# A decaying head's sum of squares by two products of rounded operands instead of one in fp32, one slot later

## The reference

```python
def _hgrn2(q_raw, f_raw, i, lb, o_g):
    q = jax.nn.silu(q_raw)
    logf = jnp.log(lb + (1.0 - lb) * jax.nn.sigmoid(f_raw))
    k = (1.0 - lb) * jax.nn.sigmoid(-f_raw)
    ...                                   # scan over chunks: o = inter + intra
    o = _rms(o, o_g)                      # o * rsqrt(mean(o * o over the head's 128) + 1e-6) * o_g
    return o
...
hg = _hgrn2(g_q, g_f, g_i, lbs[l], hg_norm_g[l]) * jax.nn.silu(g_z)
```

## Time and profile before

| | |
|---|---|
| median of three runs | 2654.63 us |
| profiled execution, its own time | 2656.35 us |
| its span, first to last instruction | 2655.04 us |
| mean granted TensorE clock, share of full | 0.997 |
| busy share: TensorE products | 99% |
| busy share: TensorE weight loads | 79% |
| busy share: VectorE | 37% |
| busy share: ScalarE | 41% |
| busy share: GpSimd | 44% |

### The profile page before, as it was taken

The page is one execution under the profiler, slowest core; times in us unless marked ns, Lnnn a source line. Parts: engine busy times, 40 slices in busy tenths (PEclk is TensorE's granted clock), DMA queues, the critical chain, the costliest instruction groups (busy, mean ns, idle before and its releaser), DMA issues.

```text
span 2655.0 us, 34587 instructions
## 1 busy us (share of the span) xinstructions
PE 2621.5 (99%) x14142; PEld 2101.7 (79%) x14142; DVE 970.0 (37%) x1584; ACT 1094.4 (41%) x1781; POOL 1162.1 (44%) x590
## 2 busy tenths in 40 slices
PE   7999999999999999999999999999999999999999
PEld 4577778778888888878887777777888888888887
DVE  3535544333334231244676333334332233321300
ACT  5335344434444442244444444445444444433311
POOL 0024344344444454453344444445555556554543
PEclk9999999999999999999999999999999999999999
DMA  9942333233333224422222323332333333333443
GB/s 386 351 156 96 103 103 106 85 122 107 115 115 106 89 99 156 146 91 80 88 80 80 104 93 103 99 107 92 105 114 115 113 108 117 115 117 110 139 146 107
DMA packets 102253, 322.92 MB, mean 122 GB/s; under 512 B 11472, under 2 KB 13264, under 8 KB 101584
## 3 DMA queue, kind: packets, MB, share of 16 engines
q1 hardware_dynamic: 98208, 307.06, 35.0%
q10 hardware_dynamic: 3888, 13.66, 1.3%
HBM read 303.90 MB, written 16.78 MB: 121 GB/s over the span
## 4 chain that ended last, share of the span: by engine, by line
PE 96%; DMA 2%; ACT 0%; DVE 0%; SPq 0%; issue 0%; POOL 0%; DVEq 0%; ACTq 0%
PE bank L813 29%; PE bank L815 28%; PE bank L814 28%; DMA TA<-in_w_ada 2%; PE bank L1020 1%; PE bank L1009 1%; PE bank L713 1%; PE bank L940 1%; PE bank L1003 1%; PE bank L974 1%; PE bank L1055 1%; PE bank L1069 0%; PE bank L880 0%; PE bank L866 0%; PE bank L1047 0%; PE bank L867 0%
## 5 line engine op out<-in xcount | busy, mean ns | idle before, releaser
L2131 POOL TENSOR_TENSOR wlo<-wraw,whi 128x1024 fp32r<-128x1024 f32 (+3 forms) x430 | 992.0, 2308 | 1358.3 <-ACT whi L1124 1357.8
L813 PE MATMUL bank<-Hhi,whi 128*128 128x512 f32 x2848 | 1147.9, 403 | 3.1 <-DVE Y L1686 1.5
L814 PE MATMUL bank<-Hlo,whi 128*128 128x512 f32 x2848 | 1111.6, 390 | 0.0
L815 PE MATMUL bank<-Hhi,wlo 128*128 128x512 f32 x2848 | 1111.5, 390 | 0.0
L1124 ACT ACTIVATE whi<-wraw 128x1024 fp32r<-128x1024 f32 (+3 forms) x454 | 457.3, 1008 | 661.0 <-PE bank L815 635.7
L813 PEld LDWEIGHTS bank<-Hhi,whi 128*128 128x128 f32 x2848 | 535.0, 188 | 132.8 <-issue 22.3
L815 PEld LDWEIGHTS bank<-Hhi,wlo 128*128 128x128 f32 x2848 | 534.7, 188 | 114.8
L814 PEld LDWEIGHTS bank<-Hlo,whi 128*128 128x128 f32 x2848 | 535.5, 188 | 107.5 <-issue 2.4
L813 PE MATMUL bank<-Ohi,whi 128*128 128x512 f32 x320 | 128.0, 400 | 0.0
L815 PE MATMUL bank<-Ohi,wlo 128*128 128x512 f32 x320 | 124.8, 390 | 0.0
L814 PE MATMUL bank<-Olo,whi 128*128 128x512 f32 x320 | 124.7, 390 | 0.0
(11 more groups left out here) (270 smaller groups left out, 2549.7 us busy)
## 6 DMA issues: line engine op xcount, KB each, us to landing
wraw<-in_w_in SPq DMA_DIRECT2D x304, 512.0 KB, 3.5
TA<-in_w_ada SPq DMA_DIRECT2D x64, 512.0 KB, 7.4
wraw<-in_w_out SPq DMA_DIRECT2D x32, 512.0 KB, 3.5
wraw<-in_w_o SPq DMA_DIRECT2D x32, 512.0 KB, 3.5
wraw<-in_w_mem ACTq DMA_DIRECT2D x16, 512.0 KB, 7.0
Y<-in_w_ada SPq DMA_DIRECT2D x16, 512.0 KB, 4.4
first<-in_w_ada SPq DMA_DIRECT2D x16, 512.0 KB, 4.6
tmp_mgs<-TA SPq DMA_DIRECT2D x32, 256.0 KB, 2.2
```

Of the source, the lines that this page charges most:

```text
L813: e.matmul(out, hi[:, c], xhi[k], start=first and j == 0, stop=False)
L814: e.matmul(out, hi[:, c], xlo[k], start=False, stop=False)
L815: m = e.matmul(out, lo[:, c], xhi[k], start=False, stop=last and end)
L2131: e.tensor_tensor(M.wlo[b][:, 0:w], M.wraw[b][:, 0:w], M.whi[b][:, 0:w].bitcast(F32), ALU.subtract).then_inc(S.lo)
```

## The change

The squares in `hg_sq` are copied by ScalarE into a rounded high part, `hg_hi`, in slot 10; VectorE subtracts it from them in slot 11, in place, to make `hg_lo`; and TensorE sums both parts with the rounded ones into the same bank in slot 12. Ln, Exp and VectorE's two products move to slot 12 too, and `hg` has 12 rests on the other engines. The high part lies in the `ST` buffer of the head's half, so the next writers of that buffer get waits: `decay` of head h waits for the sum of head h - 2, and SyncE's strips 0 and 1 wait for the sums of heads 6 and 7, where they waited for the last multiplications of heads 6 and 7.

```diff
+        self.hg_hi, self.hg_lo = pieces(TR, 6144, 2), TR[:, 4864:5376]
...
# tensor_program, hg
             yield
-            pe.wait_ge(S.hgq, h + 1)
+            yield
+            pe.wait_ge(S.hgd, h + 1)
             pe.wait_ge(*free[BS0])
-            e.matmul(M.bS0, ones, M.hg_sq, start=True, stop=True).then_inc(S.hgs)
+            e.matmul(M.bS0, one, M.hg_hi[b], start=True, stop=False)
+            e.matmul(M.bS0, one, M.hg_lo, start=False, stop=True).then_inc(S.hgs)
...
# scalar_program, hg
         e.activation(M.hg_sq, M.bO, ACT.Square).then_inc(S.hgq)
+        act.wait_ge(S.hgq, h + 1)
+        e.activation(M.hg_hi[h % 2], M.hg_sq, ACT.Copy).then_inc(S.hgh)
+        yield
         yield
         act.wait_ge(S.hgs, h + 1)
...
# vector_program, decay
             dve.wait_ge(S.t2e, t2 - 1)
+            if h > 1:
+                dve.wait_ge(S.hgs, h - 1)
             e.tensor_scalar(F, M.t2, a, M.par[:, 56 + h:57 + h], ALU.mult, ALU.add).then_inc(S.dec)
...
# vector_program, hg
         yield
+        dve.wait_ge(S.hgh, h + 1)
+        e.tensor_tensor(M.hg_lo, M.hg_sq, M.hg_hi[b].bitcast(F32), ALU.subtract).then_inc(S.hgd)
+        yield
         y = M.y[8 + h]
...
# gpsimd_program
-        gates=gates, hg=idle(11), ...
+        gates=gates, hg=idle(12), ...
...
# sync_program
     def hg(h):
         if h == 7:
-            sp.wait_ge(S.hgu, 9 * 7)
+            sp.wait_ge(S.hgs, 7)
             strip(1, 0)
-        return rest(11)
+        return rest(12)
...
             if which == 1 and h < 7:
-                sp.wait_ge(*((S.s1, 4 * h) if h else (S.hgu, 9 * 8)))
+                sp.wait_ge(*((S.s1, 4 * h) if h else (S.hgs, 8)))
                 strip(1, h + 1)
```

More of the change, by code:

```diff
@@ L433, in __init__ @@
         self.hgo, self.hgq, self.hgs, self.hgl, self.hgr = sem("hgo"), sem("hgq"), sem("hgs"), sem("hgl"), sem("hgr")
+        self.hgh, self.hgd = sem("hgh"), sem("hgd")
         self.y = sem("y")
@@ L2250, in gpsimd_program @@
         setup=setup, mem=mem, mem_kv=idle(3), mem_turn=idle(2), ada=nothing, sums=nothing, gain=nothing, h_put=h_put,
-        gates=gates, hg=idle(11), attend=attend, window=window, put=put, x_load=nothing, h2=h2, index=idle(3), topk=idle(48), mix_load=nothing, out_load=nothing, end=nothing,
+        gates=gates, hg=idle(12), attend=attend, window=window, put=put, x_load=nothing, h2=h2, index=idle(3), topk=idle(48), mix_load=nothing, out_load=nothing, end=nothing,
         part=part, out=out, posts=dict(
```

## The result

The changed kernel takes 2659.41 us (median of 20 runs, 2656.12 to 2663.13); the kernel before, run beside it, 2656.30 us (20 runs, 2654.04 to 2658.95). The ratio is 1.0013, with a 95% interval of 1.0007 to 1.0019. I had forecast 2651.7 us, 0.11% less than the 2654.63 us of three earlier runs of the kernel before; what its 20 runs show is 1.7 us above these three, so the forecast is compared by the difference: 2.9 us less forecast, 3.1 us more measured. The changed kernel's profiled execution has a span of 2659.1 us, 4.1 us more than that of before.

What follows compares the result with a forecast made beforehand. TensorE, busy 99% of the span, was taken as the bound. Seven heads saving 0.42 us each, head 7's saving lost, gave 2.9 us off 2654.63: 2651.7 us, 0.11% less; range 2650.5 to 2655.8.

Steps and rivals of the forecast that it cites:

- The step moved by one slot: `hg`, 12 rests for 11: heads 0 to 3 start 0 to 3 slots later, from head 4 only the last step shifts; cost zero.
- The saving of the products: TensorE, eight heads: fp32 sum costs 0.87 us, the rounded pair 0.45; 0.42 us saved each, 3.4 us in all.
- The chain of the remainder: Heads 4 to 6: remainder follows Square, Copy and decay tail; head 4's done at 416.2, TensorE at 416.50, no wait.
- what I said of the cover: Square, Copy and remainder have two slots (5.2 us) of cover; with one (2.73 us) every head would wait.
- Head 7: Later Ln delays the remainder of ak's norm (L1798); TensorE waits at L866, so head 7's 0.42 us saving is gone.
- The waits of decay and of SyncE: New waits of VectorE's L1784 and SyncE's strips for earlier heads' sums: zero cost.
- The rival with GpSimd: Heads 4 to 6: remainder falls behind GpSimd's subtraction, TensorE waits 3.1 us each; 2660.9 us. Chance 0.05, half collision 0.08.
- the lost saving: Rival: the pair costs what the fp32 sum did, through changing forms; 2654 to 2655 us. Chance 0.06.

Runs made afterwards that it cites:

- the experiment: The whole change without its extra slot (remainder in slot 10, pair in slot 11, 11 rests), against the kernel before: 2652.39 us, ratio 0.9984.

## Why the prediction was wrong

**The step that failed** is "The step moved by one slot", with its end "Nothing to pay". It had the new starts of heads 0 to 3 right (0, 1, 2 and 3 slots later), and then looked only at the bank that the next head needs. For the moved last step I asked what it would now stand behind on each engine's queue. For the steps in slots 0 to 10 of heads 1 to 3, which move too, I did not ask it. Those steps are links of a chain between TensorE and VectorE: each of VectorE's multiplications has to be done before TensorE comes to the next slot. The shift put them behind other work of VectorE and under GpSimd's subtraction. "From head 4 on nothing shifts but the last step" was right by the count of slots, and yet head 4 has a wait of 1.0 us, since head 3 now ends right ahead of it. What the step put at nothing cost 5.7 us of waits and 1.6 us of half clock in the profile, and 7.5 us of stage when the empty slot was tried alone.

**The saving of the products** was right: 0.42 us each forecast, 0.45 measured, 3.6 us in all eight where I had 3.4. The 131 ns of the Trainium skill ("TensorE: Matmul & The Clock Gate", "Back-to-back issue gap") are again not what the trace shows (0.23 us, 235.10 to 235.33).

**The chain of the remainder** in heads 4 to 6 was right: for head 4 I had its start 4.3 us after the Square and found 4.20 (416.82 to 421.02), and TensorE did not wait. GpSimd's subtraction began 1.07 us behind it (422.09), where I had said 1.0 us of room. All eight remainders took 0.69 us; none fell under GpSimd:

```profile
L1950 DVE TENSOR_TENSOR TR<-TA,TR x8: 684/688/693, 231.8 to 579.2; 128x512 fp32r<-128x512 f32 x8
```

**But what I said of the cover was wrong**: "if it were one (2.73 us) every head would wait". With one slot no head waits. The rows give it: Square, Copy and remainder took 1.98 us from the first start to the last end in the experiment (408.30 to 410.28), and the slot comes 2.53 us after the Square's start. I had counted the three operations and not set their sum against one slot.

**Head 7** came as worked out. Its pair is at 583.20; L1955 follows at 2.04 us (2.06 forecast), L1808 at 3.44 (3.5), L869 at 4.18 (4.2), a wait of about 1.0 us for TensorE where it had been 0.6:

```profile
583.20 0.39 PE L985 MATMUL bank<-TR,one 128*128 128x512 f32 x1
585.24 0.75 DVE L1955 SCALAR_TENSOR_TENSOR Y<-bank,cst,TA 128x512 f32<-128x512 f32 x1 [5.31 <-ACT TA L1437]
586.64 0.68 DVE L1808 TENSOR_TENSOR TR<-TA,TR 128x512 fp32r<-128x512 f32 x1
587.38 0.50 PE L869 MATMUL bank<-TR,one 128*128 128x512 f32 x1 [0.84 <-DVE TR L1808]
```

**The waits of decay and of SyncE** cost TensorE nothing, as said: its list has no row for either, and the first strip is issued at 537.36, 7.7 us behind head 6's pair.

**The rival with GpSimd** had the mechanism and the wrong victim. I looked for the collision only where an instruction was new (the remainder in heads 4 to 6) and gave it 5%; it struck old instructions in heads 2, 3 and 4. That its time (2660.9 us) lies near the measured 2659.41 is luck: it stood for three waits of 3.1 us at other instructions. The rule of the Trainium skill that I named there ("SBUF — State Buffer", "SBUF: two separate sides") is borne out by the experiment in which GpSimd's work is cut short, and by the ends: L1944, L1922 and L1924 ended 0.28 to 0.29 us behind GpSimd's subtraction (362.93 and 362.65, 387.02 and 386.74, 291.48 and 291.19). Which of the several things that stand ahead of L1941 in head 3 would have been enough by itself (the decay's tail, the gate's multiply-add) was not tried.

**A slip in the range**: its upper end, from 2655 us for the lost saving and half of 1.3, is 2655.65 and not 2655.8.

## What to carry to other kernels

Where several queues follow one plan of slots, an added slot moves all the work behind it in that line, up to the next point where the line is empty: list every step that moves, with what will stand ahead of it on its own engine, before looking at the step itself. First ask whether the slot is needed: add up the chain and set it against the slot that is there, and put the new instruction ahead of other work in its queue. A chain that must close within one slot is at risk from the long VectorE operations that come to stand ahead of it and from a GpSimd subtraction that starts just before one of its links (0.41 us became 2.56). Such a collision can turn on a tenth of a microsecond, and each of the two shifts that were tried here, by one slot and by two, brought its own.

## What I had not expected of the hardware

A wait of TensorE costs more than its length once it is long: after 3.0 us of halt the granted clock was 0.55 in the mean of 3.4 us, which took 1.6 us more; the same was seen in the second profile of the same kernel (0.52 from 360.42 to 363.67), behind the 3.0 us in the kernel with one empty slot (0.50 from 364.16 to 367.28) and behind a wait of 1.7 us in the kernel with two empty slots, while behind waits of 1.0 us the clock stayed at 1.00 and the pitch at 0.23 us. What decides between them no run here shows. And the start of this kernel varies by about as much as the whole effect (the first group of head 0 lies from 3.2 us earlier to 1.1 us later than in the trace of before, over the ten profiles), so the lateness within a stage told more than the medians.
